# Pair results stored by indirect DMAs that skip slots without a token, in a fused two-block kernel on one Trainium2 core

## The chip, the cores and the metric

The kernel runs on 1 of the cores of one Trainium2 chip. The metric is the device time of one execution in microseconds (us), taken as the median over runs. Everything is float32; 512 tokens of width 1024 pass through two transformer-like blocks in a single launch.

## The reference, cut to what matters

```
x = first_block(x, ...)       # norm, SSD mixer + chunk attention, w_out; then a conv FFN of width 2816
x = second_block(x, ...)      # windowed attention + mLSTM, merge, w_out; then hier_moe

def hier_moe(h, ...):         # T = 512 tokens, 32 experts in 4 groups, top 2
    g = argmax(h @ w_rg + b_rg)                          # one group per token
    top_v, top_i = top_k(e_logits[g], 2)                 # two experts of the group
    w = softmax(top_v) * p_group
    # 1024 (token, expert) assignments are sorted by expert into rows
    ys[row] = (silu(xb @ w_gate[e]) * (xb @ w_up[e])) @ w_down[e]
    y[token] += ys[row] * w
```

The expert weights are 32 x 3 slabs of 2 MB. With the inputs of the reference, counted by the two expert choices that it makes for each token, the 32 experts get 10 to 63 tokens each, 1024 together.

## The kernel before, in words

**Block 1** ends its projections with the output projection (`if on("wout")` on TensorE, L1015): eight groups G_WA .. G_WA+7, each of which increments `dense_full` when it is complete. VectorE adds each to the residual (L1869). Then comes the norm (L706, L713 on TensorE; L1885 to L1891 on VectorE) and the conv FFN: 11 slabs of `w_up`, each 2 MB and each computed with seven quarter products instead of eight, twice (u = 0, 1), so 14 products a slab (`up_slab`, L1041). The quarter products of u = 0 go to banks 0 to 3 and those of u = 1 to banks 4 to 7. VectorE puts the quarters together (function `slab`, L1934 to L1956) into the buffer `Cu` and ends with an increment of `up_sum`. Slab n, half u on TensorE waits for `up_sum` >= 2n + u - 1, so slab 1 starts when slab 0's half u = 0 has been put together. SyncE loads the next slab of `w_up` when TensorE has finished a slab (L533), and the first slab of `w_down` when the last G_WA group is complete (L524).

`Cu` covers columns 15360 to 16383 of the tile `arena`, and the 256 zeros of the tile `zero` stand in its columns 16128 to 16383. GpSimd writes these zeros at the start (L2924) and copies them by DMA into rows of the scratch tensor `ys_d` (3072 x 1024, in HBM) at L2942, for the rows from 1920 on: 9 DMAs of 128 rows. So VectorE waits for the semaphore `zeroed` before it first touches `Cu` (L1996, ahead of the first call of `slab`).

**The expert stage.** Experts are taken in pairs p = 0 .. 15. Each expert has 64 slots, a pair 128, and slot s of expert e is row 64e + s of `ys_d`. The tokens of an expert fill its slots from 0 on; VectorE works out each assignment's row (`R["sl"]`) and the count of each expert (`R["ct"]`). For a pair TensorE picks its tokens out of all 512 by a product with a 0/1 matrix (`pick_rows`, L1458), then multiplies by the gate and the up slabs and, after the product with silu, by the down slabs (`both_k`, L1449, 32 records each for gate, up and down). Weights arrive in a ring of nine 2 MB buffers; SyncE issues the next slab when a product has released one (L609). ScalarE copies the pair's 128 x 1024 results from PSUM to `ysb` (L2877, L2880), and for pairs 0 to 14 stores them with one DMA of 512 KB into `ys_d` (L2883). It writes `ysb` for the next pair only when that store has landed (semaphore `y_st`, L2876). An expert with more than 64 tokens gets further blocks (rows 2048 on, `block_of`).

At the end GpSimd waits for the 15 stores and gathers, by eight indirect DMAs (L2957), the two rows of each token, which VectorE multiplies by their weights and adds (L2514). Rows of pair 15 do not go through `ys_d`: a last product with the matrix `wpT` adds them (L1548, L2520).

The order of the work is written out by hand on each engine, with semaphores between engines.

Of the kernel before, what the change touches and what calls it, by code (L numbers as in the profile page):

```python
# [22 lines left out]
ALU = mybir.AluOpType  # L23
ACT = mybir.ActivationFunctionType
AX = mybir.AxisListType.X
ds = bass.ds

P = 128
# [19 lines left out]
E = 32  # L48
EF = 512
CAP = 64  # L50
OVB = (2 * T) // CAP - 1
ROWS = 3072
# [37 lines left out]
def two_blocks(nc, a, out, dbg=None, stop="end"):  # L90

    ctx = ExitStack()
    with ctx:
# [31 lines left out]
        smi = sb("smi", [P, 64], I32)  # L125
# [228 lines left out]
        G_WA = groups(8, "V")  # L354
# [36 lines left out]
        for name, shape in (("lg", (NT, 36)), ("gs", (NT, 4)), ("ge", (NT, 4)), ("g1", (NT, 4)), ("r4", (4,)), ("io", (E,)),  # L391
                            ("gm", (NT,)), ("gx", (NT,)), ("pg", (NT,)), ("em", (NT, E)), ("top", (NT, 8)), ("ix", (NT, 8)),
                            ("d", (NT,)), ("w1", (NT,)), ("ed", (NT,)), ("oh1", (NT, E)), ("oh2", (NT, E)), ("ohs", (NT, E)),
                            ("rk", (NT, E)), ("ct", (E,)), ("nb", (E,)), ("t1", (E,)), ("cin", (E,)), ("adj", (E,)),
                            ("fs", (NT, E)), ("t2", (NT, E)), ("sl", (2, NT)), ("be", (OVB + 1, E)), ("bx", (OVB + 1,)),
                            ("i15", (OVB + 1,)),
                            ("la", (NT, 36)), ("g7", (7,)), ("cm", (E, 7)), ("pre", (NT, E)), ("bs", (E,)), ("row", (P,)), ("slo", (2, NT))):
            R[name] = view(arena, r_at, *shape)
            r_at += int(np.prod(shape))
        assert r_at <= W, r_at  # L400
        wt = sm(2, NT)
        io_i = smi[:, 0:32]
        slot_i = smi[:, 32:40]

        e2 = view(arena, 15360, 512)
        rs = view(arena, W - 512, 512)
# [1153 lines left out]
        def _(ve):  # L1560
# [12 lines left out]
            def seq(ins):  # L1573

                tell(ins, "vseq")
                own("vseq")
# [304 lines left out]
            if on("ffn"):  # L1881
# [111 lines left out]
                def placed(u, p):  # L1993
                    return 7 * u + UPS.index(p) + 1

                ve.wait_ge(S["zeroed"], 16 * (ROWS - (E - 2) * CAP) // P)  # L1996
                base = [arrived["up0"][1], arrived["up1"][1]]
                slab(0, 0, (landed[1], base[1]), placed_first, early=True)
                slab(1, 1, (landed[0], base[0] + 16), placed)
# [275 lines left out]
            if on("merge"):  # L2275
                def wo_sums(u, *which):

                    w, s = slot((2, 1)[u // 2], KD, 512)[:, :, 256 * (u % 2):256 * (u % 2) + 256], wos[u % 2]
                    q = [[w[:, 4 * k:4 * k + 4, P * m:P * m + P] for k in range(2)] for m in range(2)]
                    ve.wait_ge(*arrived[f"wo2_{u // 2}"])  # L2280
                    for i in which:
                        a_, b_, op = ((q[1][0], q[1][1], ALU.add), (s[0], q[0][0], ALU.subtract), (q[0][0], q[1][0], ALU.subtract),
                                      (q[0][1], s[1], ALU.subtract))[i]
                        if i in (1, 3):
                            own("seven_s")
                        tell(ve.tensor_tensor(s[i], a_, b_, op), "seven_s")

                u00, u01, u10, u11 = (uT[:, 4 * k:4 * k + 4, 256 * t:256 * t + 256] for k in range(2) for t in range(2))

                def u_sum(i):  # L2290

                    own("u_rdy")
                    own("seven_t")
                    to, a_, b_ = ((u01, u01, u00), (wot[0], u11, u01), (wot[1], wot[0], u00), (wot[2], u10, wot[0]))[i]
                    tell(ve.tensor_tensor(to, a_, b_, ALU.subtract), "seven_t")

                def wo_part(u, p):

                    m, half = QUARTER[p]
                    n, t = 2 * u + m, HALF[half]  # L2300
                    assert done["seven_free"] + 1 == at7("wo", u, p)
                    ve.wait_ge(S["seven_full"], at7("wo", u, p))
                    own("seven_free")
                    tell(ve.tensor_tensor(xT[:, n, t], bank[wo_bank(u, p)][:, 0:256], xT[:, n, t], ALU.add), "seven_free")

                def route_tables():

                    seq(ve.tensor_copy(R["io"], io_i))
                    seq(ve.tensor_scalar(R["r4"], R["io"][:, 0:4], -1.0, 4.0, ALU.mult, ALU.add))
                    seq(ve.tensor_scalar(R["g7"], R["io"][:, 0:7], float(CAP), float(CAP), ALU.mult, ALU.add))  # L2310
                    seq(ve.tensor_scalar(R["bs"], R["io"], -float(CAP), float(CAP * (E - 1)), ALU.mult, ALU.add))
                    seq(ve.tensor_scalar(R["t1"], R["io"], float(CAP), None, ALU.mult))
                    for b in range(P // E):
                        ins = ve.tensor_scalar(R["row"][:, b * E:(b + 1) * E], R["io"], float(b * E), None, ALU.add)
                    seq(ins)
                    ve.memset(R["fs"][:, 0, :], 0.0)
                    ve.memset(R["be"][:, 0, :], 0.0)
                    ve.tensor_tensor(mn[:, 0:36], ident[:, 0:36], ident[:, 64:100], ALU.add)
                    seq(ve.memset(lgw[:, :], 0.0))

                def square_added(n):

                    ve.wait_ge(S["sq_part"], 3 * KD + n + 1)
                    own("sq_used")
                    tell(ve.tensor_tensor(sqr[0], sqr[0], sqr[n], ALU.add), "sq_used")

                wo_sums(0, 0, 1, 2, 3)
                ve.wait_ge(S["ld_small"], 32)
                tell(ve.tensor_tensor(w_rt[:, :, :], w_rt[:, :, :], blast(col("norm2", 0, 8), 36), ALU.mult), "wr_rdy")
                for m in range(KD):  # L2330
                    if m == 4:
                        u_sum(0)
                    mg = mgM2[m // 4][:, m % 4, :]
                    ve.wait_ge(*emptied(GM[m]))
                    ve.wait_ge(S["dense_full"], BM[m] + 1)
                    tell(ve.tensor_tensor(mg, mg, bank[home[BM[m]]][:, :], ALU.mult), "dve_free")
                    own("dve_free")
                    tell(ve.tensor_tensor(uT[:, m, :], mgA[:, m, :], mg, ALU.add), "u_rdy")
                u_sum(1)
                wo_part(0, 0)  # L2340
                u_sum(2)
                wo_part(0, 4)
                u_sum(3)
                wo_part(0, 1)
                wo_part(0, 5)
                for u, p in WO[4:]:
                    wo_part(u, p)
                    if (u, p) == (1, 2):
                        route_tables()
                    if (u, p) in ((0, 2), (0, 6), (1, 5), (1, 6), (2, 5), (2, 2)):  # L2350
                        wo_sums(u + 1, *((0, 1) if p in (2, 5) and (u, p) != (2, 2) else (2, 3)))
                    if (u, p) in ((2, 0), (2, 4), (3, 0), (3, 4), (3, 2), (3, 6)):
                        square_added({(2, 0): 1, (2, 4): 2, (3, 0): 3, (3, 4): 4, (3, 2): 5, (3, 6): 6}[u, p])
                    if (u, p) == (3, 4):
                        ve.wait_ge(S["lg_full"], 1)
                        tell(ve.tensor_copy(lgw[64:100, :], bank[4][64:100, :]), "lw_ev")
# [82 lines left out]
            if on("end"):  # L2439
# [58 lines left out]
                seq(ve.tensor_tensor(R["w1"], R["w1"], R["pg"], ALU.mult))  # L2498
                seq(ve.reciprocal(wt[:, 0, :], R["w1"]))
                seq(ve.tensor_tensor(wt[:, 1, :], wt[:, 0, :], R["ed"], ALU.mult))  # L2500
                picks(1)
                pair(0, True, False)
                picks(2)
# [19 lines left out]
        def _(ac):  # L2523
# [339 lines left out]
            if on("end"):  # L2863
                def pair(p, first, last):
# [13 lines left out]
                    if last:  # L2878
                        ins.then_inc(S["yy_ev"], 1)
                    nc.scalar.activation(ysb[:, 512:D], bank[7][:, :], ACT.Copy).then_inc(S["yy_ev"], 1)  # L2880
                    if not last:
                        ac.wait_ge(S["yy_ev"], p + 1)
                        ac.dma_start(ys_d[ds(p * P, P), :], ysb[:, :]).then_inc(S["y_st"], 16)  # L2883

                ac.wait_ge(S["ov_step"], 1)
                n_more = ac.value_load(smi[0:1, 40:41], min_val=0, max_val=OVB)
# [26 lines left out]
        def _(po):  # L2913
# [15 lines left out]
                             pattern=[[-1, P]], channel_multiplier=1)  # L2929
            po.memset(xraw[:, :, 0:3], 0.0)  # L2930
            po.iota(io_i, [[1, E]], base=0, channel_multiplier=0)
            for m, step, mul, op in ((tri, 1, -1, ALU.is_ge), (trib, -1, 1, ALU.is_ge), (tris, 1, -1, ALU.is_gt)):
                ins = po.affine_select(out=m[:, :], in_=ones[:, :], compare_op=op, fill=0.0, base=0, pattern=[[step, P]],
                                       channel_multiplier=mul)
# [3 lines left out]
            po.memset(T1[0:HD, :, 3 * HD:4 * HD], NEG).then_inc(S["bias1"], 1)  # L2938

            po.wait_ge(S["consts"], 1)  # L2940
            for r0 in range((E - 2) * CAP, ROWS, P):
                po.dma_start(ys_d[r0:r0 + P, :].rearrange("p (b d) -> p b d", d=256), bmid(zero, 4)).then_inc(S["zeroed"], 16)  # L2942
            if on("proj2"):
                po.wait_ge(S["seven_full"], len(DN))
# [5 lines left out]
                po.dma_start(kaS[0:HD, :], qaT[HD:P, 4, :]).then_inc(S["swapped"], 16)  # L2950
                po.dma_start(kaS[HD:P, :], qaT[0:HD, 4, :]).then_inc(S["swapped"], 16)
            if on("end"):
                po.wait_ge(S["zeroed"], 16 * (ROWS - (E - 2) * CAP) // P)
                po.wait_ge(S["y_st"], 16 * (E // 2 - 1))
                for t in range(NT):
                    for b in range(2):
# [86 lines left out]
```

## Time and profile before

| what | value |
|---|---|
| median of 3 runs | 1757.92 us (1756.85 to 1757.97) |
| the profiled execution, its own time | 1757.99 us |
| span of its records | 1756.3 us |
| TensorE busy | 1699.2 us, 97% of the span |
| VectorE, ScalarE, GpSimd busy | 44%, 18%, 1% |
| moved by DMA | 335.62 MB, of it 18.37 MB written to HBM |

The span goes from the first record to the last one; the execution's own time is 1.7 us longer. TensorE is busy nearly throughout, but a busy share is an average over stages: in the last quarter the DMA engines are as busy as TensorE is, and which of the two ends last has to be read there.

### The profile page before, as it was taken

To read this page: it belongs to the slowest core of one execution; us is meant where nothing else is said; L and a number is where in the kernel's file an instruction comes from. 1 tells how busy PE (TensorE), PEld (TensorE's weight loads), DVE (VectorE), ACT (ScalarE), POOL (GpSimd) and SP (SyncE) were. 2 spreads that over 40 slices of the span, in tenths; PEclk is the share of its full clock that TensorE was granted. 3 is DMA by queue.
4 is the path that set the end of the run, shared out by engine and by line. 5 is a ranking of instruction groups with operands and counts; after the bars stand their busy time and mean duration, and the time that the engine had idled before them with its cause. 6 is when DMAs were issued, how large, how long until landed. Compare 5 with 4: busy or idle time off the path is not lost.

```text
span 1756.3 us, 19957 instructions
## 1 busy us (share of the span) xinstructions
PE 1699.2 (97%) x7904; PEld 1053.8 (60%) x7904; DVE 774.1 (44%) x1709; ACT 324.4 (18%) x683; POOL 18.7 (1%) x39
## 2 busy tenths in 40 slices
PE   8999999999999999999999999999899999999996
PEld 5445544488888888878544445447745455444452
DVE  4322438577777782354796233325422121111123
ACT  1121224231111100120234234200200000000000
POOL 0001000000000000000000000000000000000001
PEclk9999999999999999999999999999899999999999
DMA  9874120022122213141211110433379999999997
GB/s 403 333 283 159 62 94 3 1 81 88 61 91 96 81 66 132 49 159 54 96 49 48 49 48 1 149 139 144 146 307 429 428 429 429 428 430 429 429 428 316
DMA packets 30248, 335.62 MB, mean 191 GB/s; under 512 B 3208, under 2 KB 5784, under 8 KB 10592
## 3 DMA queue, kind: packets, MB, share of 16 engines
q1 hardware_dynamic: 22464, 310.56, 43.5%
q10 hardware_dynamic: 5168, 14.91, 2.2%
q0 software_dynamic: 2544, 9.18, 1.5%
q8 instruction: 47, 0.77, 0.2%
q14 instruction: 25, 0.20, 0.0%
HBM read 319.66 MB, written 18.37 MB: 192 GB/s over the span
## 4 chain that ended last, share of the span: by engine, by line
PE 83%; DMA 8%; DVE 6%; ACT 2%; issue 1%; POOL 0%; SPq 0%; DVEq 0%; ACTq 0%; POOLq 0%
PE bank L1041 15%; PE bank L1449 14%; PE bank L1089 8%; PE bank L1458 6%; PE bank L1224 5%; PE bank L648 4%; DMA pool<-in_w_expert_up 4%; PE bank L852 3%; PE bank L1232 3%; PE bank L1133 3%; PE bank L1401 3%; PE bank L1182 3%; DMA arena<-in_w_expert_up 2%; PE bank L997 2%; PE bank L630 2%; PE bank L842 2%
## 5 line engine op out<-in xcount | busy, mean ns | idle before, releaser
L1449 PE MATMUL bank<-pool,arena 128*64 128x512 f32 x1216 | 334.6, 594 | 9.1 <-DMA pool<-in_w_expert_up 3.6
L1041 PE MATMUL bank<-pool 128*128 128x256 f32 x1232 | 267.8, 381 | 0.8 <-ACT pool L2527 0.8
L1041 PEld LDWEIGHTS bank<-pool 128*128 128x128 f32 x1232 | 235.2, 191 | 33.2 <-issue 1.0
L1449 PEld LDWEIGHTS bank<-pool,arena 128*64 128x64 f32 x1216 | 107.0, 137 | 175.2 <-issue 167.7
L2454 DVE TENSOR_TENSOR arena<-arena,bank 128x512 f32<-128x512 f32 x16 | 11.0, 687 | 280.6 <-PE bank L1449 280.6
L1458 PEld LDWEIGHTS bank<-arena 128*128 128x128 f32 x1024 | 119.4, 195 | 18.2 <-issue 12.2
L1458 PE MATMUL bank<-arena 128*128 128x128 f32 x1024 | 123.7, 280 | 5.9 <-DVE arena L2419 5.9
L1224 PE MATMUL bank<-pool 128*128 128x512 f32 x256 | 114.5, 595 | 1.9 <-DVE arena L2219 1.9
L1224 PEld LDWEIGHTS bank<-pool 128*128 128x128 f32 x256 | 47.4, 190 | 58.4 <-issue 55.0
L1449 PE MATMUL bank<-xT,arena 128*64 128x512 f32 x160 | 70.6, 594 | 4.0 <-DMA pool<-in_w_expert_up 4.0
L1449 PE MATMUL bank<-arena 128*64 128x512 f32 x160 | 70.4, 593 | 0.0
L2446 DVE TENSOR_TENSOR arena<-bank,cols 128x512 f32<-128x512 f32 x32 | 22.1, 692 | 103.7 <-PE bank L1458 103.7
L648 PE MATMUL bank<-pool 128*128 128x512 f32 x144 | 63.8, 597 | 0.0
L1182 PE MATMUL bank<-pool 128*128 128x512 f32 x128 | 60.7, 609 | 1.2 <-ACT arena L2527 1.2
L2711 ACT ACTIVATE arena<-arena,cols 128x512 f32<-128x512 f32 x44 | 29.4, 714 | 172.6 <-DVE arena L1956 172.6
L1089 PE MATMUL bank<-arena,pool 128*128 128x256 f32 x264 | 58.4, 379 | 0.0
L852 PE MATMUL bank<-pool 128*128 128x512 f32 x128 | 56.7, 593 | 0.0
L1089 PEld LDWEIGHTS bank<-arena,pool 128*128 128x128 f32 x264 | 50.2, 190 | 6.8
L2527 ACT ACT_TABLE_LOAD x39 | 50.0, 1283 | 19.6 <-DVE small L1666 17.0
L1863 DVE TENSOR_TENSOR pool<-pool 128x1024 f32<-128x1024 f32 x44 | 52.7, 1219 | 0.3
L2527 ACT ACTIVATE arena<-bank 128x512 f32<-128x512 f32 (+4 forms) x62 | 29.1, 490 | 117.0 <-PE bank L648 39.5
L2527 ACT ACTIVATE pool<-bank 128x512 f32<-128x512 f32 (+3 forms) x73 | 31.5, 463 | 95.8 <-PE bank L852 45.2
(419 smaller groups left out, 2175.7 us busy)
## 6 DMA issues: line engine op xcount, KB each, us to landing
pool<-in_w_expert_gate SPq DMA_DIRECT2D x27, 2048.0 KB, 25.9
pool<-in_w_expert_down SPq DMA_DIRECT2D x27, 2048.0 KB, 28.0
pool<-in_w_expert_up SPq DMA_DIRECT2D x22, 2048.0 KB, 25.1
pool<-in_w_in SPq DMA_DIRECT2D x15, 2048.0 KB, 8.3
pool<-in_w_ada SPq DMA_DIRECT2D x12, 2048.0 KB, 18.9
pool<-in_w_up SPq DMA_DIRECT2D x11, 2048.0 KB, 8.0
arena<-in_w_expert_gate SPq DMA_DIRECT2D x5, 2048.0 KB, 29.9
xT<-in_w_expert_up SPq DMA_DIRECT2D x5, 2048.0 KB, 24.9
```

Of the source, the lines that this page charges most:

```text
L648: ins = pe.matmul(bank[home[g]][:, :], w[:, k, c0:c0 + P], src[:, k, :], start=(k == 0), stop=(k == KD - 1))
L852: ins = pe.matmul(bank[home[g0 + c]][:, :], w[:, k, c * P:(c + 1) * P], hT[:, k, :], start=(k == 0), stop=(k == KD - 1))
L1041: ins = pe.matmul(up_quarter(u, p), lhs[:, k, :], rhs[:, k, :], start=(k == 0), stop=(k == 3))
L1089: ins = pe.matmul(dst, lhs[:, i, :], rhs[:, i, :], start=(i == 0 and p in (0, 1, 4)), stop=(i == HP - 1), skip_group_check=p not in (0, 1, 4))
L1133: ins = pe.matmul(bank[qa_bank(u, p)][:, 0:256], lhs[:, k, :], rhs[:, k, :], start=(k == 0 and p in (0, 1, 4)), stop=(k == 3), skip_group_ ...
L1182: ins = pe.matmul(bank[home[g0 + t]][:, :], hT[:, k, t * P:(t + 1) * P], w[:, k, :], start=(k == 0), stop=(k == KD - 1))
L1224: ins = pe.matmul(bank[home[g]][:, :], w[:, k, o:o + P], hT[:, k, :], start=(k == 0), stop=(k == KD - 1))
L1232: ins = pe.matmul(bank[home[g]][:, :], w[:, k, m * P:(m + 1) * P], src[:, k, :], start=(k == 0), stop=(k == 3))
L1449: ins = pe.matmul(dst[b * CAP:(b + 1) * CAP, :], lhs(b, k), rhs(b, k), start=(k == 0), stop=(k == n_k - 1))
L1458: ins = pe.matmul(bank[x][:, f * P:f * P + n], xtok[:, t, c], pick[:, t, 0:n], start=(t == 0), stop=(t == NT - 1))
L1863: return ve.tensor_tensor(sv[i], a_, b_, op)
L2527: ins = nc.scalar.activation(dst, src, f, **kw)
```

## The change

1. Pairs 0 to 14 are stored by GpSimd instead of ScalarE, with an indirect DMA each, whose row numbers come from the tile `store_i`, one for each of the 128 slots. A slot without a token has its row number raised by 4096, which is over the bound (3071), and is not stored.
2. `store_i` is filled by GpSimd with the rows' numbers (one more iota), and VectorE raises those of empty slots: two small instructions in `route_tables`, four behind the weights `wt`, ahead of `picks(1)`.
3. All 3072 rows of `ys_d` are zeroed: 24 DMAs instead of 9. GpSimd now starts them when `dense_full` has reached G_WA + 8. VectorE's wait for `zeroed` ahead of the first `slab` counts all 24.

```diff
-                            ("i15", (OVB + 1,)),
+                            ("sb", (E // 2,)), ("rr", (1,)), ("st", (E // 2,)),
...
+        store_i = smi[:, 44:44 + E // 2]
+        NOWHERE = 4096.0
...
-                ve.wait_ge(S["zeroed"], 16 * (ROWS - (E - 2) * CAP) // P)
+                ve.wait_ge(S["zeroed"], 16 * (ROWS // P))
...
                     seq(ve.tensor_copy(R["io"], io_i))
+                    seq(ve.tensor_copy(R["sb"], store_i))
+                    seq(ve.tensor_scalar(R["rr"], R["sb"][:, 0:1], -float(CAP), None, ALU.add))
...
                 seq(ve.tensor_tensor(wt[:, 1, :], wt[:, 0, :], R["ed"], ALU.mult))
+                held = R["ct"].rearrange("p (q two) -> p q two", two=2)
+                ve.tensor_scalar(R["st"][0:CAP, :], held[0:CAP, :, 0], R["sb"][0:CAP, 0:1], None, ALU.is_le)
+                seq(ve.tensor_scalar(R["st"][CAP:P, :], held[CAP:P, :, 1], R["rr"][CAP:P, 0:1], None, ALU.is_le))
+                seq(ve.scalar_tensor_tensor(R["st"], R["st"], NOWHERE, R["sb"], ALU.mult, ALU.add))
+                seq(ve.tensor_copy(store_i, R["st"]))
                 picks(1)
...
                     nc.scalar.activation(ysb[:, 512:D], bank[7][:, :], ACT.Copy).then_inc(S["yy_ev"], 1)
-                    if not last:
-                        ac.wait_ge(S["yy_ev"], p + 1)
-                        ac.dma_start(ys_d[ds(p * P, P), :], ysb[:, :]).then_inc(S["y_st"], 16)
...
             po.iota(io_i, [[1, E]], base=0, channel_multiplier=0)
+            po.iota(store_i, [[P, E // 2]], base=0, channel_multiplier=1)
...
             po.wait_ge(S["consts"], 1)
-            for r0 in range((E - 2) * CAP, ROWS, P):
+            po.wait_ge(S["dense_full"], G_WA + 8)
+            for r0 in range(0, ROWS, P):
                 po.dma_start(ys_d[r0:r0 + P, :].rearrange("p (b d) -> p b d", d=256), bmid(zero, 4)).then_inc(S["zeroed"], 16)
...
             if on("end"):
-                po.wait_ge(S["zeroed"], 16 * (ROWS - (E - 2) * CAP) // P)
+                po.wait_ge(S["zeroed"], 16 * (ROWS // P))
+                for p in range(E // 2 - 1):
+                    po.wait_ge(S["yy_ev"], p + 1)
+                    po.indirect_dma_start(ys_d, bass.IndirectOffsetOnAxis(ap=store_i[:, p:p + 1], axis=0), ysb[:, :], None,
+                                          bounds_check=ROWS - 1, oob_is_err=False).then_inc(S["y_st"], 16)
                 po.wait_ge(S["y_st"], 16 * (E // 2 - 1))
```

On GpSimd, from the last instruction of the set-up to the end of the program, before (`ys_d` is the scratch, `smi` holds row numbers, `pool` and `xT` are where the gathered rows go):

```order
L2938 MEMSET arena 64x8x64 [waits bias1]
L2942 DMA ys_d<-arena 512x1x256 [waits consts]
L2942 DMA ys_d<-arena 512x1x256 x8
L2945 MEMSET arena 128x8x2 [waits seven_full]
L2946 MEMSET arena 128x16
L2947 MEMSET arena 128x8x2
L2950 DMA arena<-arena 64x512 [waits qn_rdy]
L2951 DMA arena<-arena 64x512
L2957 DMA pool<-ys_d,smi 128x1024 [waits y_st,zeroed]
L2957 DMA xT<-ys_d,smi 128x1024
```

and now:

```order
L2945 MEMSET arena 64x8x64 [waits bias1]
L2950 DMA ys_d<-arena 512x1x256 [waits dense_full,consts]
L2950 DMA ys_d<-arena 512x1x256 x23
L2953 MEMSET arena 128x8x2 [waits seven_full]
L2954 MEMSET arena 128x16
L2955 MEMSET arena 128x8x2
L2958 DMA arena<-arena 64x512 [waits qn_rdy]
L2959 DMA arena<-arena 64x512
L2964 DMA ys_d<-arena,smi 3072x1024 [waits yy_ev,zeroed]
L2964 DMA ys_d<-arena,smi 3072x1024 [waits yy_ev] x14
L2969 DMA pool<-ys_d,smi 128x1024 [waits y_st]
L2969 DMA xT<-ys_d,smi 128x1024
```

The zeroing has 24 DMAs instead of 9 and waits for `dense_full`, and 15 indirect stores stand ahead of the gathers.

On ScalarE, the body of the loop over pairs and the last pair, before:

```order
L2868 ACTIVATE arena<-bank 128x512 [waits he_rdy,g_full]
L2873 ACTIVATE arena<-bank 128x512 [waits ht_full]
L2876 REGISTER_ALU [waits yy_full]
L2877 ACTIVATE arena<-bank 128x512 [waits y_st]
L2880 ACTIVATE arena<-bank 128x512
L2883 ISA [waits yy_ev]
L2883 DMA ys_d<-arena 128x1024
L2908 REGISTER_ALU
```

and now:

```order
L2877 ACTIVATE arena<-bank 128x512 [waits he_rdy,g_full]
L2882 ACTIVATE arena<-bank 128x512 [waits ht_full]
L2885 REGISTER_ALU [waits yy_full]
L2886 ACTIVATE arena<-bank 128x512 [waits y_st]
L2889 ACTIVATE arena<-bank 128x512
L2914 REGISTER_ALU
```

The store and the wait for `yy_ev` have left ScalarE; its wait for the landing of the pair's store before (`y_st`) stands where it stood.

## Rows read from the trace of the kernel before

**Rows 1.** The page: the span in 40 equal slices, DMA share and rate.

```profile
DMA  9874120022122213141211110433379999999997
GB/s 403 333 283 159 62 94 3 1 81 88 61 91 96 81 66 132 49 159 54 96 49 48 49 48 1 149 139 144 146 307 429 428 429 429 428 430 429 429 428 316
```

**Rows 2.** Busy time of each engine, PE clock, DMA share, GB/s, expert stage.

```profile
core 0: us, PE busy (x) PEld busy (x) DVE busy (x) ACT busy (x) POOL busy (x), PEclk, DMA share, GB/s
1296.00:1524.00 228.00, 228.00 (x1313) 115.44 (x1312) 39.19 (x104) 18.24 (x32) 0.00 (x0) 1.00 1.00 425
1538.00:1691.00 153.00, 143.91 (x824) 72.31 (x821) 27.26 (x73) 11.99 (x21) 0.00 (x0) 1.00 1.01 429
```

**Rows 3.** The chain that ended last: start us, us, what.

```profile
1288.46 3.77 PE bank L1458 x32
...
1296.23 20.75 PE bank L1449 x96
...
1324.77 20.75 PE bank L1449 x96
...
1629.76 7.09 PE bank L1449 x32
...
1690.97 7.09 PE bank L1449 x32
...
1705.84 7.04 PE bank L1449 x32
```

**Rows 4.** Waits of PE, 1250 to 1757 us: total, times, longest.

```profile
PE bank L1449 <- DMA pool<-in_w_expert_up: 7.6, 4, 2.1
...
PE bank L1449 <- DMA arena<-in_w_expert_up: 3.3, 2, 1.7
```

**Rows 5.** DMA issues, 1270 to 1715 us: KB each, median us to landing.

```profile
ys_d<-arena ACTq DMA_DIRECT2D x15, 512.0 KB, 10.4
```

**Rows 6.** The zeroing, line L2942, and the stretch in which it runs alone.

```profile
L2942 POOL DMA_DIRECT2D ys_d<-arena x9: 868/1162/1596, 161.4 to 166.7; - x9
...
DMA to landing us min/median/max: 4.8/8.3/11.7
...
166.00:176.00 10.00, 10.00 (x39) 5.07 (x38) 4.71 (x12) 1.27 (x2) 2.32 (x4) 1.00 1.01 329
```

**Rows 7.** Timeline from the output projection into the FFN, PE, SP, DVE.

```profile
328.04 25.48 PE L1015 MATMUL bank<-arena,pool 128*128 128x512 f32 x59
...
358.84 26.50 PE L1041 MATMUL bank<-pool 128*128 128x256 f32 x114 [0.82 <-ACT pool L2527]
...
353.56 0.33 SPq L524 DMA_DIRECT2D pool<-in_w_down  x1
385.10 24.51 SPq L533 DMA_DIRECT2D pool<-in_w_up  x2
...
369.75 0.42 DVE L1934 COPY pool<-bank 128x256 f32<-128x256 f32 x1
...
376.31 0.42 DVE L1946 TENSOR_TENSOR arena<-pool,bank 128x256 f32<-128x256 f32 x1 [1.02 <-PE bank L1041]
...
378.04 0.42 DVE L1951 TENSOR_TENSOR arena<-arena,bank 128x256 f32<-128x256 f32 x1 [0.85 <-PE bank L1041]
...
379.23 0.42 DVE L1956 TENSOR_TENSOR arena<-arena,bank 128x256 f32<-128x256 f32 x1
```

**Rows 8.** Windows of the two loads at the start of the FFN.

```profile
354.00:359.00 5.00, 2.68 (x20) 2.35 (x21) 2.21 (x8) 1.65 (x4) 0.00 (x0) 0.98 0.80 286
385.00:392.40 7.40, 7.40 (x36) 6.52 (x35) 6.23 (x13) 1.96 (x3) 0.00 (x0) 1.00 0.78 283
```

**Rows 9.** Window behind a stop of PE at 1260 us.

```profile
1264.40:1270.00 5.60, 5.53 (x26) 5.53 (x27) 0.63 (x4) 0.00 (x0) 0.00 (x0) 0.50 0.03 9
```

**Rows 10.** The chain at the end of the program.

```profile
1714.31 10.58 DMA ys_d<-arena
...
1725.74 1.04 POOL pool L2957
...
1729.60 7.26 DMA xT<-ys_d,smi
```

**Rows 11.** DVE timeline ahead of picks(1), and its last instruction.

```profile
1275.62 0.16 DVE L2498 TENSOR_TENSOR arena<-arena 128x4 f32<-128x4 f32 x1
...
1279.01 0.17 DVE L2432 TENSOR_SCALAR arena<-arena 128x8 f32<-128x8 f32 x1
```

## The prediction, made before the changed kernel had run

> **What bounds the kernel.** I read the page's slices first: DMA is light in the middle and at nine tenths or more from slice 31 to slice 39, at 428 to 430 GB/s [rows 1]. So there are two regimes, and the change touches one place in each.
>
> In the expert stage the windows by stretch show that TensorE and the DMA engines are both full until about 1524 us, and that TensorE falls back to 143.91 of 153 us behind it, with DMA still full [rows 2]. The chain of waits gives the reason: two pairs start their x96 group 28.54 us apart at first (20.75 us each at L1449, the rest in L1458), which is TensorE's own pace, and later two pairs take 61.21 us (1629.76 to 1690.97), 30.6 each [rows 3]. That is the pace of the DMAs: two pairs need 12 slabs of 2.097 MB and two stores of 0.524 MB, 26.2 MB, and 26.2 MB / 61.2 us is 428 GB/s. The nine buffers let TensorE run ahead for nine pairs; then each second pair waits for its up slab. TensorE's waits for up slabs total 10.9 us, and one of 1.8 us falls in pair 15 [rows 4]. A bound for what fewer bytes can give: at TensorE's pace pair 14's last group would start at 1296.23 + 14 x 28.54 = 1695.8 us instead of 1705.84, so **10.0 us** at most up to there.
>
> At 353.5 us, where the zeroing will be put, the chain is TensorE alone: the output projection ends at 353.52, and from 358.84 the FFN's 14 quarter products of slab 0 run until 385.05 without a wait for VectorE, when SyncE sends the next slab of w_up (385.10) [rows 7].
>
> **The change, part by part.**
>
> *Removed: the first zeroing.* 9 DMAs from 161.4 us on [rows 6], beside TensorE work that waits for none of them: 0.
>
> *Added: 24 zeroing DMAs behind the output projection, and VectorE's wait for them.* This is the large term. The form is the same, so its price is read from the nine. They are issued from 161.4 on, the last at 166.7 and landed at most 11.7 us later, at 178.4: **17.0 us** for nine, with the DMA engines full and only 329 GB/s moved between 166 and 176 [rows 6]. The other 15 are 7.86 MB, at 329 GB/s **23.9 us**. The same engines carry the first slab of w_down, issued at 353.56 too, 0.80 of 5 us = **4.0 us** of all engines, and the slab of w_up issued at 385.10, 0.78 of 7.4 = **5.8 us** [rows 8]. I count both in full, less about 1 us where the fixed times overlap, since the loads share the engines with a zeroing that is not over at 385 us. From 353.6: 353.6 + 17.0 + 23.9 + 4.0 + 5.8 - 1 = **403 us** for the last landing. GpSimd issues one every 0.7 us (eight intervals from 161.4 to 166.7), faster than the 1.6 us that its bytes take, so the issue is covered.
>
> VectorE used to pass this wait at 369.75 (L1934) [rows 7]. Everything it has to do for slab 0's first half stands behind it: from 369.75 to the end of L1956 at 379.65, less its 1.02 and 0.85 us of waiting for TensorE, 8.0 us. So up_sum reaches 1 at 403 + 8 = 411 us. TensorE needs it at 385.05 and has nothing else to do: banks 0 to 3 are full. It had 5.4 us to spare here (379.65 against 385.05), which is all that the kernel can hide. **Loss: 411.0 - 385.05 = 26 us.** VectorE's second half ends some 8 us later, before TensorE needs it (seven products, about 12 us), so the stop comes once; behind it TensorE is the bound of the FFN and nothing gives the time back.
>
> *TensorE's clock behind the stop.* Behind a stop of 7 us the granted clock was 0.50 (1.2 GHz) from 1264.4 to 1270 [rows 9]: 5.6 us at half speed lose **2.8 us**. The new stop is longer, so I add 2.8.
>
> *Moved: the stores to GpSimd, with fewer rows.* Pairs 0 to 13 count up to pair 14's up slab. Counted from the reference's inputs, 856 of their 1792 slots hold a token, so 936 rows of 4096 B fall away: 3.83 MB, at 429 GB/s [rows 2] 8.9 us, if a skipped row costs nothing and its share goes evenly from all engines. Between 0 and 8.9 I take **-5 us**, near the middle, since no row of this trace shows how an indirect store is dealt out.
>
> [...] No row here shows engines apart.
>
> *The store's latency.* ScalarE waits for a store only at the next pair, 28.5 us later, and a store lands in 10.4 [rows 5]: covered, unless an indirect one takes three times as long. It counts only at the end: store 14 takes 10.58 us to land, then the gathers begin [rows 10]. The new one costs GpSimd about 1.04 us (as a gather) instead of 0.34 on ScalarE, with fewer packets; a gather lands in 7.26. Between -3.3 and +0.7 I take **-1 us**.
>
> *VectorE's small instructions.* Six of about 0.16 to 0.2 us [rows 11]. Four stand ahead of picks(1), which ends at 1279.2 and is needed at 1288.46 [rows 3]: 9 us of cover, 0. The two in route_tables stand in the output projection's stretch with waits around them: 0. The iota: 0.
>
> **Sum:** 26.0 + 2.8 - 5 - 1 = +22.8. Against the profiled execution's 1757.99 us that is 1780.8; the median of the runs is 0.07 lower. I give **1780 us**.
>
> **Rivals.**
> *A: the zeroing goes at the stream's rate.* In the expert stage the engines move 429 GB/s with stores among the loads [rows 2]. At that rate 12.58 MB take 29.3 us; with 2.7 us of fixed time (17.0 - 4.72 MB / 329 GB/s) and 4.0 for w_down it ends at 389.6, about 391 with part of the next slab; the stop is 391 + 8 - 385 = 14 us, and with +2.8 and -6 the time is 1769. Against it: the nine of this very form had the engines full at 329 GB/s. Chance 10%. [...]
>
> *B: slower still.* The loads keep the zeroing back more than their bytes, GpSimd is held up while VectorE is busy, and skipped rows save nothing: Z = 408, stop 31, +2.8, 0 from the stores, +0.7: 1792. Chance 10%.
>
> *C, the other side: the stop is hidden and the saved rows decide.* If the rows are zeroed by 377 us (385.05 - 8.0), TensorE never notices, and 8.9 + 1 us of store bytes and latency make 1748. For that 12.58 MB must go in 23.4 us, 538 GB/s, over every rate on the page. It turns faster than before at a stop under some 6 us, a landing before 383 us. Chance 4%.
>
> *D: the wait is where I put it, but the stores do nothing* (out-of-range rows are still carried, or the engine with the low slots sets the pace): +28.8, or 1787. Chance 16%, within my range.
>
> My forecast has 60%.
>
> **How the numbers follow.** A measurement can tell about 0.2%, 3.5 us. Faster: only C, 0.04. Same: a stop of 5 to 10 us, 0.03, between C and A. Slower: 0.93. The range takes in A's upper part and D and leaves out C and the end of B: 1768 to 1790.
>
> **What would show it.** Right: in the timeline a stop of TensorE between L1041 records from about 385 to 411 us; VectorE waiting for a DMA ys_d<-arena ahead of L1934; clock 0.5 behind it; DMA share full from 354 to 403. In the expert stage an ys_d queue on GpSimd with about 945 rows instead of 1920 (pairs 0 to 14), pairs under 30.6 us apart and fewer waits for up slabs. Wrong: L1934 starting before 385 us, or a landing of the zeroing before 390; then A or C holds. If pairs 10 to 14 keep 30.6 us, D holds.

## The result, and the profile after

The changed kernel takes **1782.85 us** (median; 1782.70 to 1783.04) against 1757.95 us: the ratio is 1.0142, 95% interval 1.0123 to 1.0161, so 24.9 us slower. 1780 was predicted, within 1768 to 1790. The profiled execution has a span of 1781.0 us, 24.7 more than before.

The timeline of the changed kernel around the new zeroing, for GpSimd, VectorE, TensorE and SyncE (start us, us, engine, line, what, and the idle time before with its releaser):

```profile
352.76 17.99 POOL L2950 DMA_DIRECT2D ys_d<-arena  x24 [191.30 <-PE bank L1017]
...
402.81 0.42 DVE L1936 COPY pool<-bank 128x256 f32<-128x256 f32 x1 [34.49 <-DMA ys_d<-arena]
...
410.43 0.42 DVE L1958 TENSOR_TENSOR arena<-arena,bank 128x256 f32<-128x256 f32 x1
...
357.44 27.25 PE L1043 MATMUL bank<-pool 128*128 128x256 f32 x112 [0.70 <-ACT pool L2536]
411.00 29.32 PE L1043 MATMUL bank<-pool 128*128 128x256 f32 x127 [26.30 <-DVE arena L1958]
...
384.88 52.72 SPq L535 DMA_DIRECT2D pool<-in_w_up  x2
```

Against [rows 7]: VectorE came to its copy at the same point of its work (here 368.3) and now waits 34.49 us for the zeroing's last landing. 8.0 us after it has begun, it has put the first half together, and TensorE starts slab 1 at 411.00, having stood for **26.30 us**. SyncE's load of the next slab goes out at 384.88, in the middle of the zeroing.

The windows (wall time, busy time of the engines, PE clock, DMA share, GB/s) show what the DMA engines do in that time:

```profile
356.00:366.00 10.00, 9.30 (x33) 7.54 (x32) 8.97 (x19) 6.49 (x16) 10.00 (x17) 0.66 1.00 363
366.00:376.00 10.00, 10.00 (x48) 8.81 (x47) 2.29 (x2) 0.00 (x0) 4.75 (x7) 1.00 1.01 330
376.00:386.00 10.00, 8.69 (x41) 7.31 (x39) 0.00 (x0) 0.00 (x0) 0.00 (x0) 1.00 1.01 328
386.00:396.00 10.00, 0.00 (x0) 0.00 (x0) 0.00 (x0) 0.00 (x0) 0.00 (x0) 0.55 1.03 338
...
411.00:413.00 2.00, 2.00 (x5) 1.64 (x6) 1.32 (x2) 1.98 (x3) 0.00 (x0) 0.50 0.00 0
413.00:415.00 2.00, 2.00 (x8) 1.65 (x7) 1.93 (x4) 1.15 (x2) 0.00 (x0) 0.65 0.00 0
415.00:417.00 2.00, 2.00 (x11) 1.77 (x10) 1.86 (x5) 0.00 (x0) 0.00 (x0) 1.00 0.00 0
```

The engines are full and move 328 to 330 GB/s where the zeroing runs alone, the rate of the nine before [rows 6]. TensorE had been idle for 26.30 us before 411.00; the granted clock is 0.50 right behind that, 0.65 in the next two microseconds, and 1.00 from 415 us on.

Both loads fall into the zeroing. Between 352 and 404 us the queues carried (packets, MB, share of 16 engines; `q0` the zeroing, `q1` the loads):

```profile
q0 software_dynamic: 3456, 12.58, 71.1%
q1 hardware_dynamic: 288, 3.54, 19.8%
```

In the expert stage the chain now reads:

```profile
1325.83 20.75 PE bank L1451 x96
...
1354.36 20.75 PE bank L1451 x96
...
1611.12 13.91 PE bank L1451 x64
1625.04 29.27 DMA pool<-in_w_expert_up
...
1683.15 32.28 DMA arena<-in_w_expert_up
...
1730.43 7.04 PE bank L1451 x32
...
1739.44 11.14 DMA ys_d<-arena,smi
```

From pair 0's x96 group to pair 14's x32 group it takes 404.60 us (1325.83 to 1730.43); before, 409.61 (1296.23 to 1705.84) [rows 3]. The first up slab that the chain has to wait for is issued at 1625.04, and its product starts at 1654.36, 328.5 us behind the first x96 group. Before, the product of the first such slab started at 1568.78, 272.6 us behind that group: two pairs earlier.

So the 24.7 us are: the stop 26.30; the stage from pair 0 to pair 14 -5.01; the tail behind it +0.11 (50.57 instead of 50.46 us to the end of the span); and +3.3 in several stretches of TensorE work whose instructions are the same. The last part splits into five: -1.40 ahead of the FFN; +1.05 in slab 0; +2.05 in the FFN behind the stop (243.64 for 241.59 us up to the start of the next loop, L1091); +2.77 in block 2 up to the expert stage; and -1.17 at its first picks.

### The profile page after: what moved, and what is told of

Read it like the earlier page. It is cut to its first block, busy times and chain, and to the rows that moved or that the text cites. A ratio compares the mean times of both kernels' runs of the same rounds, so it can differ in the third digit from the quotient of the medians.

```text
span 1781.0 us, 19965 instructions
## 1 busy us (share of the span) xinstructions
PE 1699.8 (95%) x7904; PEld 1055.3 (59%) x7904; DVE 775.1 (44%) x1715; ACT 324.2 (18%) x683; POOL 44.5 (2%) x70
## 4 chain that ended last, share of the span: by engine, by line
PE 82%; DMA 8%; DVE 6%; ACT 2%; issue 1%; POOL 1%; SPq 0%; DVEq 0%; ACTq 0%; POOLq 0%
PE bank L1451 15%; PE bank L1043 14%; PE bank L1091 7%; PE bank L1460 6%; PE bank L1226 5%; PE bank L650 4%; PE bank L854 3%; PE bank L1234 3%; PE bank L1135 3%; PE bank L1403 3%; PE bank L1184 2%; DMA ys_d<-arena 2%; DMA arena<-in_w_expert_up 2%; PE bank L999 2%; DMA pool<-in_w_expert_up 2%; PE bank L632 2%
## 5 line engine op out<-in xcount | busy, mean ns | idle before, releaser
L1043 PE MATMUL bank<-pool 128*128 128x256 f32 x1232 | 270.9, 383 | 27.0 <-DVE arena L1958 26.3
L1043 PEld LDWEIGHTS bank<-pool 128*128 128x128 f32 x1232 | 237.1, 193 | 60.6 <-issue 27.6
L1091 PE MATMUL bank<-arena,pool 128*128 128x256 f32 x264 | 58.4, 379 | 0.0
L1091 PEld LDWEIGHTS bank<-arena,pool 128*128 128x128 f32 x264 | 50.2, 190 | 6.8
L1091 PE MATMUL bank<-pool 128*128 128x256 f32 x220 | 49.1, 379 | 0.0
## 6 DMA issues: line engine op xcount, KB each, us to landing
pool<-in_w_expert_down SPq DMA_DIRECT2D x27, 2048.0 KB, 24.7
```

What stands on the lines that cost most here:

```text
L1043: ins = pe.matmul(up_quarter(u, p), lhs[:, k, :], rhs[:, k, :], start=(k == 0), stop=(k == 3))
L1091: ins = pe.matmul(dst, lhs[:, i, :], rhs[:, i, :], start=(i == 0 and p in (0, 1, 4)), stop=(i == HP - 1), skip_group_check=p not in (0, 1, 4))
```

## The experiments

What separates the theories is where zeroing is started, who waits for it, and which rows a store carries. All line numbers are those of the changed kernel. "Pair 0 to 14" is the time from pair 0's x96 group to pair 14's x32 group in the chain. The kernel before, run beside the three groups of experiments, took 1757.6, 1757.7 and 1758.1 us.

**The zeroing put back to its old place.**

```diff
-            po.wait_ge(S["dense_full"], G_WA + 8)
             for r0 in range(0, ROWS, P):
```

> The change with its 24 zeroing DMAs started where the nine started before (about 161 us), all else as in the change. Theory (VectorE's wait behind a late start stops TensorE, the stores themselves gain): the stop of 26.3 us and the slow clock behind it (2 to 4 us) go, and 5 to 6 us of saved store rows stay: 1752 to 1754 us. Rival 1 (zeroing costs its DMA time wherever it stands, since loads behind it come late): over 1765. Rival 2 (the stores gain nothing, the 4 to 6 us seen at the end come from elsewhere): 1758.

1753.6 us, ratio 0.9976 (0.9967 to 0.9985), 4.0 us less than before. Pair 0 to 14 takes 404.80 us. The stop has gone: TensorE does the FFN's 1232 products of L1043 without one. Both rivals fall. Without the late start nothing of the loss is left, and the zeroing does not cost its DMA time wherever it stands (e_all_rows below, with the same 24 DMAs at 161 us and all rows stored, takes the time of before).

**The zeroing part alone**, with the direct stores on ScalarE:

```diff
+                    if not last:
+                        ac.wait_ge(S["yy_ev"], p + 1)
+                        ac.dma_start(ys_d[ds(p * P, P), :], ysb[:, :]).then_inc(S["y_st"], 16)
...
-                for p in range(E // 2 - 1):
-                    po.wait_ge(S["yy_ev"], p + 1)
-                    po.indirect_dma_start(ys_d, ...)
```

> The zeroing part alone: 24 DMAs behind the output projection as in the change, but the pairs stored by ScalarE with direct DMAs as before. Theory: the stop stays and the saved rows are lost, 5 to 6 us over the change: 1788 to 1789. Rival (stores gain nothing): 1783, as the change.

1787.84 us, ratio 1.0167 (1.0152 to 1.0183). The stop is 27.36 us. The time is 5.0 us over the change, so the stores' gain is there beside the stop too. That it is exactly 5.0 is chance. In the spans the two differ by 5.4 us: pair 0 to 14 takes 411.55 us here against 404.60, so 6.95 more, the tail behind it 48.65 against 50.57, so 1.92 less, and pair 0 starts 0.37 later.

**Half of the zeroing early, half late.**

```diff
-            po.wait_ge(S["dense_full"], G_WA + 8)
             for r0 in range(0, ROWS, P):
+                if r0 == ROWS // 2:
+                    po.wait_ge(S["dense_full"], G_WA + 8)
```

> The change with the first 12 zeroing DMAs at the old place and only the last 12 behind the output projection. Theory (the stop is the bytes of the late zeroing at 329 GB/s, less 5.4 us that TensorE has to spare): 12 fewer are 19.1 us less, and the load of w_up then comes behind it (5.8 us less): landing near 378, stop 0 to 3 us, 1752 to 1757 us. Rival (the stop is not the bytes: GpSimd's issue, or a fixed latency behind the trigger): a stop over 8 us, 1762 or more.

1754.06 us, ratio 0.998 (0.9971 to 0.9989). In its timeline:

```profile
376.85 0.43 DVE L1936 COPY pool<-bank 128x256 f32<-128x256 f32 x1 [7.97 <-DMA ys_d<-arena]
...
385.04 55.28 PE L1043 MATMUL bank<-pool 128*128 128x256 f32 x255 [1.24 <-DVE arena L1958]
```

Twelve DMAs less, and VectorE's copy starts 26.0 us earlier. The bytes of twelve are 19.1 us of that. The load of w_up goes out at 383.99, behind the landing, and no longer falls into the zeroing; that it explains most of the other 6.9 us is an estimate by the 5.8 us that the load was priced at. Of VectorE's 7.97 us of waiting only 1.24 reach TensorE. So the stop is the time to the landing less what TensorE has to spare, here 6.7 us.

**Zeroing late, but from a tile that nothing overwrites**, so that nobody waits for it at the FFN:

```diff
-                ve.wait_ge(S["zeroed"], 16 * (ROWS // P))
...
+                ve.wait_ge(S["zeroed"], 16 * (ROWS // P))
                 ve.tensor_scalar(mnf, tri[:, :], -NEG, NEG, ALU.mult, ALU.add)
...
             po.wait_ge(S["dense_full"], G_WA + 8)
+            then(po.memset(mn[:, :], 0.0))
...
-... bmid(zero, 4)
+... bmid(mn[:, :], 4)
```

> The change with the zeroing started at the same late place, but read from a tile that nothing overwrites (mn, set to 0 there and used again only in block 2), so that VectorE has nothing to wait for ahead of its first slab. Theory (the wait is the cost, not the transfer): 1752 to 1756. Rival (the transfer keeps the loads of w_up back, and TensorE stops anyway): a stop of 5 us or more at an L1043 record waiting for a DMA or for VectorE's slab sums, 1760 or more.

1754.28 us, ratio 0.9979 (0.997 to 0.9988). In its timelines TensorE goes through, and VectorE waits 2.00 us for the slab of w_up, which lands late:

```profile
358.21 81.96 PE L1043 MATMUL bank<-pool 128*128 128x256 f32 x372 [0.82 <-ACT pool L2536]
...
398.60 2.48 DVE L1865 TENSOR_TENSOR pool<-pool 128x1024 f32<-128x1024 f32 x2 [2.00 <-DMA pool<-in_w_up]
```

The same 12.58 MB go out at the same place (GpSimd issues them from 353.65 on): without the wait they cost nothing that can be measured, 1754.28 us against 1753.6 with the early start. What cost 26 us was that `zero` and `Cu` share columns of `arena`, and that VectorE therefore had to wait.

**All rows stored, by indirect DMAs.** From here on the zeroing is early.

```diff
-        NOWHERE = 4096.0
+        NOWHERE = 0.0
```

> Early zeroing (as e_early24), indirect stores, but no slot's row number is raised, so all 128 rows of a pair are stored. Theory (the gain is the skipped rows): pairs return to 30.6 us apart once the ring has run dry, and the time is 5 to 6 us over e_early24's. Rival (the gain comes from having the store on GpSimd's queue, not from the rows): as e_early24.

1757.52 us, ratio 1.000 (0.999 to 1.001), 3.9 us over e_early24, where 5 to 6 were expected; pair 0 to 14 takes 409.34, 4.54 more. Moving the store to GpSimd's queue is worth nothing (1757.52 us against 1757.7 before); the gain is the skipped rows.

**No row stored** (the experts' part of the output is missing but for pair 15):

```diff
-                ve.tensor_scalar(R["st"][0:CAP, :], held[0:CAP, :, 0], R["sb"][0:CAP, 0:1], None, ALU.is_le)
-                seq(ve.tensor_scalar(R["st"][CAP:P, :], held[CAP:P, :, 1], R["rr"][CAP:P, 0:1], None, ALU.is_le))
+                seq(ve.tensor_scalar(R["st"], held[:, :, 0], 0.0, None, ALU.is_ge))
```

> Early zeroing, indirect stores in which every row is out of range, so that no pair's results are stored and the gathers bring zeros (the experts' part of the output, but for pair 15, is left out). It gives the whole price of the stores. Weights alone need 12.58 MB a pair, 29.3 us at 429 GB/s, over TensorE's 28.54: the ring runs dry only near the last pairs, so theory: up to 10 us faster than all rows, 3 to 5 us faster than e_early24. Rival (a skipped row costs as much as a stored one): as e_early24 and e_all_rows.

1745.17 us, ratio 0.993 (0.9913 to 0.9947). TensorE never waits for a slab in the expert stage; pair 0 to 14 takes 399.41 us, which is 14 x 28.53, its own pace. The time is 12.4 us under all rows and 8.4 under e_early24, more than the 10 and the 3 to 5 that were expected. The expectation had the ring of buffers run dry near the last pairs, and it did not: against e_early24 pair 0 to 14 is 5.4 us shorter, the tail 2.4, and the start of pair 0 lies 1.1 earlier, which is within the scatter of that start. What a skipped row costs can be read from the DMA queues between 1270 and 1715 us (packets, MB, share of 16 engines), first with no rows, then with all rows:

```profile
q0 software_dynamic: 2160, 0.01, 0.3%
```

```profile
q0 software_dynamic: 2016, 7.34, 4.0%
```

A skipped row still is a packet (144 a store in both, 15 and 14 stores), but it moves next to nothing and takes next to no time. The rival falls.

**Which rows are stored: the same number, other slots.** Both store 64 of 128 rows a pair whatever the tokens (others are left out of the output). First slots 0 to 31 of both experts, then slots 0 to 15 and 32 to 47:

```diff
-                ve.tensor_scalar(R["st"][0:CAP, :], held[0:CAP, :, 0], R["sb"][0:CAP, 0:1], None, ALU.is_le)
-                seq(ve.tensor_scalar(R["st"][CAP:P, :], held[CAP:P, :, 1], R["rr"][CAP:P, 0:1], None, ALU.is_le))
+                sl_ = R["rr"][:, 0:1]
+                seq(ve.tensor_copy(R["rr"][0:CAP, :], R["sb"][0:CAP, 0:1]))
+                seq(ve.tensor_scalar(R["st"], sl_.to_broadcast([P, E // 2]), 32.0, None, ALU.is_ge))
```

and, in place of the last line:

```diff
+                wide = sl_.to_broadcast([P, E // 2])
+                seq(ve.tensor_scalar(R["st"], wide, 16.0, None, ALU.is_ge))
+                seq(ve.scalar_tensor_tensor(R["st"], wide, 32.0, R["st"], ALU.is_ge, ALU.subtract))
+                seq(ve.scalar_tensor_tensor(R["st"], wide, 48.0, R["st"], ALU.is_ge, ALU.subtract))
```

> Early zeroing; of every pair the slots 0 to 31 of both experts are stored, whatever their tokens, 64 rows of 128 (tokens in other slots are left out of the output). [...] Rows by blocks of 8 slots: half the engines keep 8 rows, no saving, as e_all_rows. [...]

> As e_slots_low with the same 64 rows of 128 a pair, but the slots 0 to 15 and 32 to 47 of both experts. [...] By blocks of 8 slots: no saving either, here and in e_slots_low. Rows dealt one by one over the engines: the same time as e_slots_low.

Slots 0 to 31: 1748.41 us (ratio 0.9949, 0.9933 to 0.9966), pair 0 to 14 in 401.88. Slots 0 to 15 and 32 to 47: 1758.03 us (ratio 1.0006, 0.9996 to 1.0015), pair 0 to 14 in 409.32, the same as with all rows. The ends of that stretch in the two chains, slots 0 to 31 first:

```profile
1294.98 20.75 PE bank L1451 x96
...
1696.86 7.04 PE bank L1451 x32
```

```profile
1296.32 20.75 PE bank L1451 x96
...
1705.64 7.04 PE bank L1451 x32
```

Their queues carry nearly the same between 1270 and 1715 us (15 stores of the first fall into that time, 14 of the second):

```profile
q0 software_dynamic: 2143, 3.94, 2.3%
```

```profile
q0 software_dynamic: 2016, 3.67, 2.1%
```

Half the bytes gone, and in one case 9.1 us are saved (7.5 of them between pair 0 and pair 14), in the other none: at the same number of rows it is their place that decides.
```diff
-                        ins = ve.tensor_scalar(R["row"][:, b * E:(b + 1) * E], R["io"], float(b * E), None, ALU.add)
+                        ins = ve.tensor_scalar(R["row"][:, b * E:(b + 1) * E].rearrange("p (k r) -> p k r", r=4),
+                                               R["io"].rearrange("p (r k) -> p k r", k=8), float(b * E), None, ALU.add)
...
+                    seq(ve.tensor_tensor(own_row, ident[:, :], R["row"], ALU.mult))
+                    seq(ve.tensor_reduce(R["rr"], own_row, AX, ALU.add))
+                    seq(ve.tensor_scalar(R["sb"], R["sb"], R["rr"][:, 0:1], None, ALU.add))
...
-            po.iota(store_i, [[P, E // 2]], base=0, channel_multiplier=1)
+            po.iota(store_i, [[P, E // 2]], base=0, channel_multiplier=0)
```

(An overflow block reads its columns in the old order.)

> A version meant to beat both: early zeroing, indirect stores with the empty slots skipped, and the slots of an expert dealt over the partitions so that consecutive tokens go to different engines (column 32b + 4k + r of a pair's 0/1 matrix holds slot 32b + 8r + k, and the store's row numbers follow). [...] Rival (the saving follows the sum of rows, and e_slots_16 was slow for another reason): as e_early24, 1753.6.

**1750.92 us**, ratio 0.9962 (0.9948 to 0.9975), the fastest of all that compute the whole output: 7.1 us under the kernel before, and 32 under the change. It is 2.7 us under e_early24, and e_all_rows less e_spread is 6.6. Against e_early24 the same rows are read and they go to the same places in `ys_d`; only the partitions that they are read from differ, and pair 0 to 14 is 2.6 us shorter (402.16 for 404.80). The rival, by which the time would be 1753.6, falls. In the chain the first product that waits for an up slab now starts at 1683.33 and belongs to pair 14:

```profile
1296.04 20.75 PE bank L1451 x96
...
1638.39 13.91 PE bank L1451 x64
1652.31 30.89 DMA arena<-in_w_expert_up
...
1698.20 7.04 PE bank L1451 x32
```

The whole series, with the rows stored of pairs 0 to 13 (of 1792) and what the bytes of the others would save at 429 GB/s [rows 2], an estimate:

| kernel | rows stored | saved by bytes, us | pair 0 to 14, us | less than all rows | median us |
|---|---|---|---|---|---|
| e_all_rows | 1792 | 0 | 409.34 | 0 | 1757.52 |
| e_slots_16 | 896 | 8.6 | 409.32 | 0.0 | 1758.03 |
| e_early24 | 856 | 8.9 | 404.80 | 4.5 | 1753.6 |
| e_spread | 856 | 8.9 | 402.16 | 7.2 | 1750.92 |
| e_slots_low | 896 | 8.6 | 401.88 | 7.5 | 1748.41 |
| e_no_rows | 0 | 17.1 | 399.41 (TensorE's pace) | 9.9 | 1745.17 |

The order is not that of the rows stored. 896 rows save 0.0 us in one kernel and 7.5 in another, and 856 rows save 4.5 and 7.2; in e_no_rows TensorE's pace ends the saving at 9.9.

## Why the prediction was right, point by point

**What bounds the kernel.** Right: TensorE alone at the FFN, the DMA engines late in the expert stage. The bound of 10.0 us for what fewer bytes can give up to pair 14 is what e_no_rows found: 9.9 against all rows, 10.2 against before.

**The zeroing's landing.** 403 us was forecast, 49.7 behind a start at 353.6. GpSimd started at 352.76, and VectorE's copy, which waited for the landing, at 402.81, 50.05 us later. The sum was right within half a microsecond. The rate carried over: 329 GB/s in the nine, 328 to 330 in the 24. Rival A, at 429 GB/s, is refuted by these windows. Rival B, slower still (a landing at 408, a stop of 31 us, 1792), is refuted by the landing and the stop. Counting the two loads in full was right too: between 352 and 404 us they took 19.8% of the engines' time, 10.3 us, where 4.0 + 5.8 were counted.

**The stop.** 26 us forecast, 26.30 measured, at the place and with the end (411.0) given, of which VectorE's 8 us behind the landing are part. e_own_zero shows that it is the wait and not the transfer; e_early24 and e_late12 show that the stop follows the landing.

**The clock.** 2.8 us forecast; the FFN behind the stop took 2.05 us longer than before, and 2.20 longer in e_direct_late24 (243.79 for 241.59), the other kernel with the long stop. So the term was right in kind and too large by 0.6 to 0.75 us: the clock was 0.50 in the first two microseconds, 0.65 in the next two, and full from there on, where 5.6 us at half speed had been taken over from [rows 9]. The traces give the clock as a share of full speed; no trace shows it in GHz. Slab 0 is no part of it. It lies ahead of the stop, and its +1.05 us is of the size by which equal work differs anyway: the 1232 products of L1043 take 266.95 to 269.00 us in the kernels in which they run without a stop, 267.80 before.

All that the late start costs can be taken from two comparisons in which next to nothing else differs: the change less e_early24 is 29.2 us, and e_direct_late24 less the kernel before is 30.2. Less their stops (26.30 and 27.36) that leaves 2.9 us each, of which 2.05 and 2.20 lie directly behind the stop. The forecast had 26.0 + 2.8 = 28.8 for the two terms. The rest cannot be told from scatter: pair 0's first group starts anywhere from 1294.98 to 1296.32 us in the nine kernels without the long stop. The same holds for the +2.77 us in block 2: from the start of L1091 to the picks it takes 637.8 us before and 640.6 in the change, 640.5 in e_direct_late24 and 637.9 to 640.0 in the other eight kernels.

**The stores.** -5 forecast, -5.0 measured between pair 0 and pair 14. The sign and the place were reasoned; the size was luck, the middle between two bounds, for want of a row. The cleanest comparison, e_early24 against e_all_rows, gives 3.9 by the medians and 4.5 between pair 0 and pair 14. The upper bound of 8.9, bytes in proportion, would have been 4.4 too high, and bytes alone do not settle it: e_slots_low and e_slots_16 store the same number of rows, and between pair 0 and pair 14 they save 7.5 us and none.

**The tail.** -1 forecast, between -3.3 and +0.7; +0.11 measured for the whole tail, and +1.1 for the store itself, which is outside these bounds. From the end of ScalarE's last copy to the start of the store it takes 0.54 us more than before, near the +0.7 that was allowed for GpSimd's issue. What failed is "with fewer packets; a gather lands in 7.26": the store took 11.14 us to land instead of 10.58 [rows 10], although 39 of its 128 rows were skipped (its queue moved 0.36 MB instead of 0.52). Its packets are as many as before (144), and the bytes make little difference to the landing: with no row stored it takes 9.72 us, with all rows 10.76. The tail as a whole came out near zero by chance: the part behind the landing was 1.0 us shorter, in which the last gather landed in 5.59 us instead of 7.26, and that gather takes anything from 5.59 to 7.50 in the eleven kernels.

**VectorE's small instructions** cost nothing, as said: e_all_rows, which has them all, takes the time of before.

**The rivals.** D (the stores gain nothing) is refuted by e_early24, though one of its reasons, that the engine with the low slots sets the pace, would fit with only 4.5 of 8.9 us being gained; no trace shows the engines apart. C, the other side, said that a landing before 383 us makes the change faster than before. With all 24 DMAs behind the output projection that does not happen; e_late12, with half of them there, lands at 376.8 and is 3.5 us faster than before.

**The sum.** +22.8 forecast, +24.7 in the profiled executions: 26.30 for the stop, 2.05 behind it, -5.01, +0.11, and +1.25 of scatter. Nearly all of the miss is the tail and that scatter.

## What to carry to other kernels

A buffer's last reader counts as much as its first: a constant tile that shares memory with a later buffer turns a transfer without a deadline into one with a deadline, so before moving a bulk transfer, ask who reuses its source and when, and compare its bytes at the rate of its own form with the time left. Bytes taken out of a full stream need not pay in proportion: here half the rows of each store gave 9.1 us or nothing, by which rows they were. Where the saving falls short of the bytes, try storing the part that stays from other partitions: here that gave another 2.7 us (e_spread against e_early24). Move the filler work (zeroing) to where the engines are idle and nothing is waiting: here at 161 us the 24 DMAs were free (e_all_rows, 1757.52 us against 1757.7).

## What had not been expected of the hardware

Which half of the rows of a store is skipped decided whether 9.1 us or nothing was saved, at the same number of bytes. A skipped row of an indirect store stays a packet of almost no bytes and time (2160 packets, 0.01 MB, 0.3% of the engines' time in 445 us). And a zeroing of 12.58 MB beside the FFN's own loads, with the DMA share at 0.91 to 1.02 from 353 to 393 us (e_own_zero), delayed VectorE by 2.00 us and TensorE by none when nobody waited for it.
